# Reordering ScalarE's and VectorE's work in the "even" attention stage and at the joins into two gated MLPs of a four-layer kernel

## The reference

```
for layer in range(2):
    h = rmsnorm(x, attn_norm[layer])
    if layer == 0:   # "even": 8 forget-gated (fox) heads and 8 sparse latent (dsa) heads
        proj = h @ w_in_even          # fq, fk, fv, ff, dq, ckv, dkr, iq, ik, iw
        fox  = softmax(fq @ fk / 8 + cumulative log gates, causal) @ fv
        score = sum_heads(iw * relu(iq @ ik)), causal
        sel   = the 64 best keys of each token by score
        dsa   = softmax(rope and latent scores / 8, only keys in sel) @ c_kv
        x = x + concat(fox, dsa @ w_uv) @ w_out_even
    else:            # "odd": 16 heads, one block of 256 keys
        x = x + attention(h @ w_in_odd) @ w_out_odd
    g, u = split(rmsnorm(x, ffn_norm[layer]) @ w_up)
    x = x + (silu(causal_conv3(g)) * u) @ w_down
return rmsnorm(x, final_norm)
```

## Time and profile before

| | |
|---|---|
| three runs | 1176.23, 1179.33, 1180.21 us, median 1179.33 |
| profiled execution | 1176.23 us, of which the span from first to last instruction is 1174.3 |
| mean granted PE clock | 0.998 |
| busy: PE, DVE, ACT, POOL | 1143.4, 827.7, 657.7, 130.4 us |

### The profile page before, as it was taken

How to read it: one execution, slowest core, us unless ns; L and a number is a source line. 1 busy time by engine, 2 the same in 40 slices (tenths; PEclk the granted TensorE clock), 3 DMA queues, 4 the chain that set the end, 5 groups by cost and what they waited for, 6 DMA issues and landing times.

```text
span 1174.3 us, 26672 instructions
## 1 busy us (share of the span) xinstructions
PE 1143.4 (97%) x10647; PEld 975.8 (83%) x10647; DVE 827.7 (70%) x1320; ACT 657.7 (56%) x1019; POOL 130.4 (11%) x168
## 2 busy tenths in 40 slices
PE   8989999999998999999999999999999999999998
PEld 7878888888787888888876688888887768888887
DVE  6776787755785886655668769877666666987664
ACT  7664575533666566533475658555446655756432
POOL 0000200000202200000232320000123631000010
PEclk9999999999999999999999999999999999999999
DMA  8751276555362466546452436654574343755451
GB/s 335 259 197 57 95 250 209 172 190 210 112 247 73 144 216 208 193 172 214 143 194 95 140 113 225 208 200 141 180 259 164 129 147 109 261 202 192 148 178 55
DMA packets 31468, 206.59 MB, mean 176 GB/s; under 512 B 3488, under 2 KB 3872, under 8 KB 10144
## 3 DMA queue, kind: packets, MB, share of 16 engines
q1 hardware_dynamic: 31104, 205.00, 50.9%
q10 hardware_dynamic: 288, 0.52, 0.1%
HBM read 204.46 MB, written 1.05 MB: 175 GB/s over the span
## 4 chain that ended last, share of the span: by engine, by line
PE 87%; DVE 9%; issue 1%; ACT 1%; POOL 0%; DVEq 0%; ACTq 0%
PE ps L617 21%; PE ps L618 20%; PE ps L619 20%; DVE w_lo L2218 2%; PE ps L953 2%; PE ps L738 1%; PE ps L628 1%; PE ps L1380 1%; PE ps L877 1%; PE ps L1381 1%; PE ps L1382 1%; PE ps L715 1%; PE ps L879 1%; PE ps L878 1%; PE ps L630 1%
## 5 line engine op out<-in xcount | busy, mean ns | idle before, releaser
L1463 ACT ACTIVATE w_hi<-staged 128x2048 f16<-128x2048 f32 (+2 forms) x195 | 344.9, 1785 | 238.4 <-PE ps L619 229.3
L618 PE MATMUL ps<-f_lo,w_hi 128*128 128x256 f16 x1596 | 435.0, 273 | 0.0
L617 PE MATMUL ps<-f_hi,w_hi 128*128 128x256 f16 x1596 | 435.0, 273 | 0.0
L619 PE MATMUL ps<-f_hi,w_lo 128*128 128x256 f16 x1596 | 435.0, 273 | 0.0
L2218 DVE SCALAR_TENSOR_TENSOR w_lo<-staged,w_hi 128x2048 f16<-128x2048 f32 (+2 forms) x195 | 415.0, 2142 | 23.6 <-ACT w_hi L1463 23.5
L617 PE MATMUL ps<-x_hi,w_hi 128*128 128x256 f16 x704 | 192.0, 273 | 1.2 <-DVE w_lo L2218 0.6
L619 PE MATMUL ps<-x_hi,w_lo 128*128 128x256 f16 x704 | 191.9, 273 | 0.0
L618 PE MATMUL ps<-x_lo,w_hi 128*128 128x256 f16 x704 | 191.9, 273 | 0.0
L618 PEld LDWEIGHTS ps<-f_lo,w_hi 128*128 128x128 f16 x1596 | 156.2, 98 | 19.4
L617 PEld LDWEIGHTS ps<-f_hi,w_hi 128*128 128x128 f16 x1596 | 156.2, 98 | 18.4
L619 PEld LDWEIGHTS ps<-f_hi,w_lo 128*128 128x128 f16 x1596 | 156.2, 98 | 17.9
(11 more groups left out here) (363 smaller groups left out, 1799.8 us busy)
## 6 DMA issues: line engine op xcount, KB each, us to landing
staged<-weights SPq DMA_DIRECT2D x165, 1024.0 KB, 5.2
staged<-weights SPq DMA_DIRECT2D x32, 704.0 KB, 4.3
xn<-bands SPq DMA_DIRECT2D x3, 512.0 KB, 9.6
m<-bands SPq DMA_DIRECT2D x3, 512.0 KB, 7.7
cst<-constants SPq DMA_DIRECT2D x1, 1027.0 KB, 7.8
h<-x_turned SPq DMA_DIRECT2D x2, 512.0 KB, 5.0
staged<-weights SPq DMA_DIRECT2D x2, 512.0 KB, 7.1
qT<-bands SPq DMA_DIRECT2D x2, 512.0 KB, 11.5
```

Of the source, the lines that this page charges most:

```text
L617: pe.matmul(out, wh, xh[:, c, :], start=(c == 0), stop=False)
L618: pe.matmul(out, wh, xl[:, c, :], start=False, stop=False)
L619: last = pe.matmul(out, wl, xh[:, c, :], start=False, stop=(c == kc - 1))
L1463: act.activation(w_hi[:, s, o:o + n], staged[:, s, o:o + n], ACT.Copy, scale=SW).then_inc(hi_split, 1)
```

## The change

PE's, POOL's and SP's programs stay as they are. On ACT and DVE, operations change places and one is taken out.

- Join, ACT: `split` of half 6 moves from the end of `joined` to `glu_mlp`, behind `root` and ahead of half 7. Join, DVE: half 6 moves from the end of `joined_into_h` to `glu_mlp`, behind `pair(0, 0, ...)`, that is behind L2232, L2812, L2827 and L2830 and ahead of half 7.
- Even stage, ACT: the one-element `Exp` (L1895) that stood ahead of `exp_pair(0)` is removed, and the eviction of product 9 moves ahead of `exp_pair(0)`.
- Even stage, DVE: `invert_pair(0)` moves behind the index scores (L2738 to L2743); the 8 rounds of `take`, before in groups of 4, 2 and 2, now come as 2, 2, 1 and 3, with the last three and `sel` behind `reduce_pair(3)`; the splits of halves 12, 13 and 14 each move ahead of a `rope_query` or `reduce_pair` that they followed.

```
@@ ACT, joined
                 for c in range(4, DC):
                     square(c)
-                act.wait_ge(product[name], 6)
-                split(2 * FIRST[name] + 6)
@@ ACT, even stage
-            act.activation(by_token[:, 0:1], by_token[:, 11:12], ACT.Exp)
+            even_evict(9, val[:, 0, 0:512], late_col[:, 0:1], 512)
             exp_pair("even", 0)
-            even_evict(9, val[:, 0, 0:512], late_col[:, 0:1], 512)
@@ ACT, glu_mlp
                 root(f"ffn2_{layer}")
+                split(2 * FIRST[("oute", "outo")[layer]] + 6)
                 last_behind(("oute", "outo")[layer])
@@ DVE, even stage
             even_split(8)
-            invert_pair("even", 0)
             ...
             dve.wait_ge(dots_added, 1)
+            invert_pair("even", 0)

             reduce_pair("even", 1)
             even_split(9)
             ...
+            take(0, 2)
             invert_pair("even", 1)
-            take(0, 4)
             low_pair("even", 0)
-            take(4, 6)

             reduce_pair("even", 2)
             even_split(10)
+            take(2, 4)
             invert_pair("even", 2)
-            take(6, TOPK // 8)
+            take(4, 5)
             low_pair("even", 1)
-            chain(dve.tensor_scalar(sel[:], ...))
-            chain(dve.tensor_tensor(sel[:], sel[:], k("causal"), ALU.add))

             reduce_pair("even", 3)
             even_split(11)
             add_rope_keys(0)
             invert_pair("even", 3)
+            take(5, TOPK // 8)
             low_pair("even", 2)
+            chain(dve.tensor_scalar(sel[:], ...))
+            chain(dve.tensor_tensor(sel[:], sel[:], k("causal"), ALU.add))
             rope_query(0)
-
+            even_split(12)
             reduce_pair("even", 4)
-            even_split(12)
             add_rope_keys(1)
             low_pair("even", 3)
             invert_pair("even", 4)
+            even_split(13)
             rope_query(1)
-
+            even_split(14)
             reduce_pair("even", 5)
-            even_split(13)
             low_pair("even", 4)
             invert_pair("even", 5)
             rope_query(2)
-
             reduce_pair("even", 6)
-            even_split(14)
             low_pair("even", 5)
             invert_pair("even", 6)
@@ DVE, glu_mlp
                 pair(0, 0, (False, True))
-                split(2 * FIRST[("oute", "outo")[layer]] + 7)
+                for e in range(2):
+                    split(2 * FIRST[("oute", "outo")[layer]] + 6 + e)
                 pair(0, 1)
```

More of the change, by code:

```diff
@@ L2750, in _ @@
             dve.scalar_tensor_tensor(CKV_NORMED, CKV, v("g_ckv"), stat[:, 1, :], ALU.mult, ALU.mult).then_inc(scaled, 1)
+            take(0, 2)
             invert_pair("even", 1)
-            take(0, 4)
             low_pair("even", 0)
-            take(4, 6)
             reduce_pair("even", 2)
             even_split(10)
+            take(2, 4)
             invert_pair("even", 2)
-            take(6, TOPK // 8)
+            take(4, 5)
             low_pair("even", 1)
-            chain(dve.tensor_scalar(sel[:], idx[:, TOPK // 8 % 2, :], TAKEN / 2, MASKED, ALU.is_gt, ALU.mult))
-            chain(dve.tensor_tensor(sel[:], sel[:], k("causal"), ALU.add))
             reduce_pair("even", 3)
@@ L2767, in _ @@
             invert_pair("even", 3)
+            take(5, TOPK // 8)
             low_pair("even", 2)
+            chain(dve.tensor_scalar(sel[:], idx[:, TOPK // 8 % 2, :], TAKEN / 2, MASKED, ALU.is_gt, ALU.mult))
+            chain(dve.tensor_tensor(sel[:], sel[:], k("causal"), ALU.add))
             rope_query(0)
+            even_split(12)
             reduce_pair("even", 4)
-            even_split(12)
             add_rope_keys(1)
```

## The result

| | before | after |
|---|---|---|
| median of the runs | 1178.69 us (4 runs, 1176.23 to 1180.21) | 1198.47 us (4 runs, 1194.68 to 1198.97) |
| ratio | | 1.0168, 95% interval 1.0147 to 1.0188 |
| profiled execution, its span | 1176.23, 1174.3 us | 1202.22, 1200.3 us |

The kernel is slower by 19.8 us (17.3 to 22.2 by the interval). The forecast was 1196.0 us, in the range 1187 to 1202: direction and size hold. One step of the sum does not, the term put at 0 for pairs 5 to 7, and it is the most instructive thing here.

What follows compares the result with a forecast made beforehand. PE was taken as the bound, so time moves only with its waiting. Even stage +7.8 and joins +8.9 sum to +16.7 us: 1192.9 on the profiled execution, 1196.0 on the median, range 1187 to 1202.

Steps and rivals of the forecast that it cites:

- pairs 5 to 7: Even stage, splits in other places: DVE's and PE's work equal within half a microsecond, 0 us, with up to 2.
- Pair 0: Even stage, turn_pair(0): PE newly waits 3.8 us for POOL's division, behind DVE's inversion moved after the index scores.
- The clock term, 1.3: Behind the new wait at turn_pair(0): PE's clock falls to half rate and PE loses 1.3 us.
- Half 10: Even stage, chunk 15: PE's 2.1 us wait and its half-rate stretch go, -3.8 us, with 0.5 us to spare.
- Query 0: Even stage, score_pair(4): new wait of about 4.8 us, PE 6.0 us late in place of 1.3, clock loss 0.9.
- query 1: Even stage, from query 0 to query 1: DVE needs 8.0 us where PE took 7.44; another 0.9 us taken.
- Joins: Two joins: PE waits 2.75 us for half 6 and loses 1.7 of clock at each, +8.9 us.
- rival 1: Whole kernel: the new waits don't lower the clock; sum +10.7, 1190.0 us; chance 0.2.
- Rival 2: Joins: half 6 is in time and they cost 0, only the even stage pays; +7.8, 1187.1 us; chance 0.07.
- Rival 3: Even stage: DVE becomes its bound altogether, half 10 missing its margin; +22.5, 1201.8 us; chance 0.15.
- Rival 4: Even stage: faster, half 10's wait goes and pair 0 is divided in time; 1175.5 us; chance 0.03.

Runs made afterwards that it cites:

- even_only: The changed kernel with the joins put back as before, leaving the even-stage part alone; 1191.17 us, ratio 1.0112.
- pair0_only: The kernel before with only pair 0 changed: no early exponential table load, product 9's eviction ahead of exponentials, inversion behind index scores; 1180.21 us, ratio 1.0017.
- rounds_back: even_only with DVE's order of pairs 1 to 3, all rounds of the index choice included, as in the kernel before; 1187.21 us, ratio 1.0080.
- mask_back: even_only with the last rounds, take(5, 8), and the mask put back ahead of reduce_pair(3); 1190.68 us, ratio 1.0112.
- pairs_back: even_only with the splits of halves 12, 13 and 14 around pairs 4 to 6 put back in the order before; 1185.83 us, ratio 1.0061.
- join_early: join_only with DVE splitting half 6 ahead of pair(0, 0), ACT's order staying as changed; 1179.31 us, ratio 1.0002.
- half_warm: The kernel before with 18 further unused matmuls on PE ahead of its wait for half 10; 1178.48 us, ratio 0.9998.
- improved: The kernel before with DVE's order of pairs 2 to 4 changed the other way, take(4, 6) behind invert_pair of pair 2; 1179.79 us, ratio 1.0011.
- port_one: The kernel before with three unused one-input reciprocals on DVE behind invert_pair of pair 7; one execution, 1178.52 us.
- join_only: The kernel before with only the join part changed, the moves of half 6; 1187.15 us, ratio 1.0077.
- join_warm2: join_only with 24 further unused matmuls on PE ahead of its wait for half 6 in both layers; 1183.61 us, ratio 1.0050.
- port_two: The kernel before with two unused long two-input instructions on DVE behind invert_pair of pair 7; one execution, 1180.72 us.

## Why the prediction was right, and where it was not

- **Bound by PE's waits.** Right: every part of the loss is a wait of PE or the lower clock behind one. The forecast's +16.7 stands against +19.8 (17.3 to 22.2), and +21.2 in the trace. The 4.5 us between the sum and the trace are 5.1 too little behind `score_pair(4)` and 1.0 too much at pair 0, with 0.4 elsewhere; that the error at pair 0 went the other way is luck, and so is that the median before came out 0.6 us under the one that the forecast started from: without it 1196.0 would have missed by 3.1 us and not by 2.5.
- **Pair 0.** Forecast a wait of 3.8, measured 2.7. The index scores took 3.7 us from their first row to the mask's in before (622.54 to 626.24) and 2.9 after (627.28 to 630.21): in before POOL's division of pair 0 ran beside them, after it ran behind them. So the term was taken from a stretched row, and the rest is the division, 1.90 us in place of 2.17. ACT came out as worked out: its exponentials ended at 625.3 (less the 4.83) where the forecast had 625.1, but with the scores shorter its cover was 0.7 us, not 1.7. The clock term, 1.3, was 1.5 in this execution (the distance to before grows from 7.59 us at `turn_pair(0)` to 9.13 at `out_pair(0)`), and none in the profiles of even_only and pair0_only.
- **Half 10.** The -3.8 hold: no wait of L1135, and PE, 4.3 us late at `out_pair(0)`, was 0.5 late at `score_pair(3)` (both less the 4.83). pair0_only adds that pair 0's lateness alone brings only 0.6 us of the wait; the rounds' move brought the rest (in rounds_back, with the rounds put back, 1.5 us of it return).
- **Query 0.** A wait of 4.73 where 4.8 was worked out, 5.3 us late in place of 6.0. Right, and for the reason given: the rounds lost their cover (rounds_back), while it does not matter where the mask stands (mask_back). The clock term behind it was too small: 0.9 was taken from a low stretch of 3.4 us, but the clock was low from 666.9 to 673.7, 6.8 us. PE was at work again in the last 4.7 of them, and that cost 2.3. In pairs_back, which has no other wait from there to `score_pair(6)`, the same stretch cost 2.6. With the 1.15 us of query 1 (0.9 forecast) this makes the 3.3 us of that step.
- **Pairs 4 to 7: the step that failed.** "For pairs 5 to 7 the splits stand elsewhere, but DVE's work and PE's are equal within half a microsecond; I take 0." The trace has 3.6 us there, between `score_pair(5)` and `score_pair(6)`: 1.95 of wait for POOL and 1.65 of clock. The sum counted DVE's time and not what a split does to POOL beside it: divisions of 2.08 us take 6.08 and end 1.95 us behind the moment when PE wants them, and in this execution the clock falls once more behind that. Putting the order back returns 6.0 us, query 1's wait included.

  The Trainium skill, "SBUF — State Buffer", section "SBUF: two separate sides", states the rule: VectorE and GpSimd share a pair of ports under an exclusive lock that one instruction holds to its end, and an instruction of VectorE with two SBUF inputs takes it against one of GpSimd that reads SBUF. The trace agrees (5.90 us beside two-input instructions, 1.90 beside one-input ones). By it the prediction could have asked of each moved split which division it now meets. An estimate from that rule, with durations of before's rows: behind the inversion PE wants the division after a split (2.2), a query (0.9), the scores (0.9) and some 0.2 between them, 4.2 us; held up by two splits it is done after 2.1 + 4.4 + 0.2 = 6.7. That is a wait of 2.5 us where 1.95 was measured.
- **Joins.** 2.65 us of wait and 1.7 of clock each, as worked out; 9.0 in the trace, 9.1 (6.7 to 11.4) alone. join_early shows that DVE's order is the cause: with it put back and ACT's left as changed, the time is that of before.
- **Rivals.** The clock fell behind every long new wait of the changed kernel's profile, and the interval (17.3 to 22.2) leaves out rival 1's +10.7. Rival 2 needed half 6 in time; it was 2.65 us late. Rival 3's 1201.8 is 3.3 us above what was measured, no nearer than the forecast, and its terms did not come: half 10 kept its margin. Rival 4 never came near.

**Still open.** How the 6 us that pairs_back returns divide. The two waits that go are 1.15 + 1.95 = 3.1 us. The clock behind the division is the other part that a trace shows, 1.65 us in the changed kernel's (0.58), but nothing in even_only's (1.00), whose profiled execution was the fastest of its own. And whether half_warm's fill is worth its fraction of a microsecond.

## What to carry to other kernels

Where a cross-engine chain runs over two engines, list for each moved instruction what it will run beside, not only what it runs behind: here a long two-input VectorE instruction beside GpSimd's division doubled it, and two put right behind the instruction that releases it tripled it, although GpSimd's program is unchanged. An operation that fills idle time of its engine is free only there; the rounds, moved by 10 us and more, came onto the path, with the mask in either place. And a wait that a profile shows may be paid for by slack just behind it: improved removed the wait of 2.1 us and got 3.9 us of new ones.

## What the hardware did that was not expected

- POOL's division of four times 128x128 took 1.90 us beside one-input DVE work (port_one), 2.08 to 2.09 where a query's short two-input addition ran beside it (before, pairs 4 to 6), 4.13 beside one long two-input DVE instruction (rounds_back, pair 3) and 5.90 to 6.09 beside two. Those took 2.26 to 2.48 us, against 2.29 alone. With short instructions (128x128, the index scores in before) the division took 2.17 and DVE lost too: 1.12 us for two where they take 0.75 alone.
- The clock falls behind some waits and not behind others of the same length. The same wait of 2.1 us for half 10 was followed by a low clock in the profiles of before, join_only, join_warm2 and port_one, and not in join_early and port_two. In these last two the clock had been at 0.57 and 0.60 from 96 to 104 us; in the four others at 0.79 to 1.00. The wait of 2.7 us at `turn_pair(0)` was followed by a low clock in the changed kernel and rounds_back, and not in even_only, pairs_back, mask_back and pair0_only. The Trainium skill, "TensorE: Matmul & The Clock Gate", Part 1, says that the monitor runs free of the kernel, and this would make executions differ as they do; no run here controls it. Before's own times spread from 1174.76 to 1180.38 us; whether this is the reason no run shows.
- The low stretch behind the wait for query 0 was twice as long as the one behind half 10: 6.8 us in the changed kernel against 3.4 in before.
- A wait whose releaser the profile gives as "issue" can be a full dependence: the 5.41 us of L1179 in mask_back end with DVE's reading of the bank, not with anything in PE's sequencer.
